# Squares summed by TensorE behind a stream, Down's banks in two groups, and a silu of one column ahead of each gate turn

## The reference

```python
# first_block, for l in range(2)
u = rms_norm(h, norm_pre_mix[l])
p = u @ w_in[l]                      # four mixers follow on slices of p
h = h + rms_norm(mixed @ w_out[l], norm_post_mix[l])
u = rms_norm(h, norm_pre_ffn[l])
ffn = (silu(u @ w_ffn_gate[l]) * (u @ w_ffn_up[l])) @ w_ffn_down[l]   # 2048 -> 5632 -> 2048
h = h + rms_norm(ffn, norm_post_ffn[l])
# second_block: one layer, attention of two kinds, then
x + gate * rms_norm_2(merged @ w_out, g_post)
```

## Time and profile before

| | us |
|---|---|
| median of 3 runs | 4174.72 |
| lowest, highest | 4172.66, 4178.52 |
| the profiled execution | 4183.72 |
| its span, first to last instruction | 4181.5 |
| PE busy | 3740.4 (89%) |
| PEld busy | 3315.9 (79%) |
| DVE busy | 2042.0 (49%) |
| ACT busy | 1763.6 (42%) |
| POOL busy | 1680.6 (40%) |
| mean granted TensorE clock | 0.945 |

### The profile page before, as it was taken

The page is one execution under the profiler, slowest core; times in us unless marked ns, Lnnn a source line. Parts: engine busy times, 40 slices in busy tenths (PEclk is TensorE's granted clock), DMA queues, the critical chain, the costliest instruction groups (busy, mean ns, idle before and its releaser), DMA issues. The chain is left out here.

```text
span 4181.5 us, 60673 instructions
## 1 busy us (share of the span) xinstructions
PE 3740.4 (89%) x25774; PEld 3315.9 (79%) x25774; DVE 2042.0 (49%) x2000; ACT 1763.6 (42%) x1700; POOL 1680.6 (40%) x663
## 2 busy tenths in 40 slices
PE   8788888799999998787888799999998889889988
PEld 7787787688888887776788688888887788878777
DVE  5536533555554555645532555555555433244464
ACT  4315333544443445415433544444445324544443
POOL 0425555399990000324555299993000124540000
PEclk9999899899999999998989899999999979999999
DMA  5413334477765554413334477775554623326443
GB/s 190 130 52 110 109 114 147 155 237 235 240 227 179 181 181 131 132 52 106 103 115 136 148 236 242 236 234 172 189 181 160 193 62 105 111 94 201 161 161 121
DMA packets 380728, 655.44 MB, mean 157 GB/s; under 512 B 14928, under 2 KB 192096, under 8 KB 379648
## 3 DMA queue, kind: packets, MB, share of 16 engines
q1 hardware_dynamic: 365632, 598.24, 44.0%
q0 software_dynamic: 14912, 54.53, 3.7%
HBM read 645.37 MB, written 6.29 MB: 156 GB/s over the span
## 5 line engine op out<-in xcount | busy, mean ns | idle before, releaser
L213 PE MATMUL ps<-x_parts,w_hi 128*128 128x512 f32 x6160 | 2205.2, 402 | 109.3 <-DVE w_lo L192 31.8
L184 ACT ACTIVATE w_hi<-weight_ring 128x2048 fp32r<-128x2048 f32 (+1 forms) x564 | 1065.9, 1890 | 1617.8 <-PE ps L214 1079.7
L214 PE MATMUL ps<-x_parts,w_lo 128*128 128x256 f32 x6160 | 1739.1, 282 | 0.0
L213 PEld LDWEIGHTS ps<-x_parts,w_hi 128*128 128x128 f32 x6160 | 1170.9, 190 | 414.7 <-issue 74.3
L192 DVE TENSOR_TENSOR w_lo<-weight_ring,w_hi 128x2048 fp32r<-128x2048 f32 x392 | 955.3, 2437 | 1078.9 <-ACT w_hi L184 1078.9
L192 POOL TENSOR_TENSOR w_lo<-weight_ring,w_hi 128x2048 fp32r<-128x2048 f32 (+1 forms) x172 | 791.8, 4607 | 1430.9 <-ACT w_hi L184 1430.9
L214 PEld LDWEIGHTS ps<-x_parts,w_lo 128*128 128x128 f32 x6160 | 1177.0, 191 | 0.0
L542 PE MATMUL ps<-x_parts,w_hi 128*128 128x256 f32 x2592 | 795.3, 307 | 138.6 <-POOL w_lo L192 75.4
L543 PE MATMUL ps<-x_parts,w_hi 128*128 128x256 f32 x2592 | 759.4, 293 | 0.0
L544 PE MATMUL ps<-x_parts,w_lo 128*128 128x256 f32 x2592 | 758.2, 293 | 0.0
L542 PEld LDWEIGHTS ps<-x_parts,w_hi 128*128 128x128 f32 x2592 | 524.0, 202 | 173.4 <-POOL w_lo L192 94.0
(11 more groups left out here) (393 smaller groups left out, 2637.0 us busy)
## 6 DMA issues: line engine op xcount, KB each, us to landing
weight_ring<-in_w_in SPq DMA_DIRECT2D x212, 1024.0 KB, 5.2
weight_ring<-in_w_ffn_gate SPq DMA_DIRECT2D x88, 1024.0 KB, 5.3
weight_ring<-in_w_ffn_up SPq DMA_DIRECT2D x88, 1024.0 KB, 5.2
weight_ring<-in_w_ffn_down SPq DMA_DIRECT2D x88, 1024.0 KB, 5.3
spare<-in_w_ada POOLq DMA_DIRECT2D x96, 512.0 KB, 5.0
weight_ring<-in_w_out SPq DMA_DIRECT2D x32, 768.0 KB, 4.5
weight_ring<-in_w_out SPq DMA_DIRECT2D x24, 1024.0 KB, 5.1
weight_ring<-in_w_br_a SPq DMA_DIRECT2D x8, 1024.0 KB, 5.1
```

Source lines behind the costliest of these rows:

```text
L184: core.nc.scalar.activation(core.w_hi[:, g % 2, at], core.ring[:, (self.start + g) % RING, at], ACT.Copy)\
L213: mm(out, hi, core.x_parts[:, x, :, :].rearrange("p a t -> p (a t)"), start=first, stop=False)
L214: return mm(out[:, 0:T], lo, core.x_hi[:, x, :], start=False, stop=last)
```

## The change

Three things.

*A silu of one column.* In Linear.ahead the ScalarE loop of the gate stream begins each trip with a Silu on one column of the constant ones, written to a tile "table" of its own that nobody reads.

*Down's banks in two groups.* In the first and the last slab of each half the products go group by group: banks 0 to 3 with both rows of tiles, then banks 4 to 7. The eighth product of a half's last slab raises first_banks_full; the first copy (L731) waits for that alone, the second for slab_used. VectorE no longer waits for slab_used there, only for the copies. The first slab of the second half waits for evacuated[0] ahead of its first product and for evacuated[1] ahead of its ninth.

*Squares.* Every quarter's squares get a place of their own (acc, sq, and x tiles 4 to 7 and 0 to 3), and VectorE's adds and folds are dropped. TensorE sums the squares of quarters 0, 1 and 2 in Post.tail, behind the last matmul of the stream and still in its block: 12 matmuls into bank 0, once that bank's last output has been read, the third group after a wait for quarter 2's squares. Only the four matmuls of quarter 3 are left for the next block. There ScalarE's order is now: square of quarter 3, L184 of slab 1, root, scales of quarters 2 and 3.

```diff
--- before.py
+++ after.py
@@ -289,12 +289,11 @@
                     self.post.early_square(eng, q - 1)
                     if q < 3:
                         self.post.scale(eng, q - 1, q)
-                elif self.post is not None and part == "low" and q == 2:
-                    self.post.early_sum(eng)
-                    self.post.fold(eng)
 
         if self.ahead_trips > 0:
             with eng.Fori(0, self.ahead_trips) as i:
+                if part == "high" and self.kind == "gate":
+                    self.core.nc.scalar.activation(self.core.table[:, :], self.core.const("ones")[:, 0:1], ACT.Silu)
                 for g in range(BODY):
                     step(g, i)
         for g in range(max(self.ahead_trips, 0) * BODY, self.n_slabs):
@@ -416,6 +415,9 @@
                             chunk(q, i)
                 for q in range(trips * self.body, self.total):
                     chunk(q, None)
+                if post is not None:
+                    pe.wait_ge(core.free[0].sem, core.free[0].base + (self.total - 2) // 2 + 2)
+                    post.tail(pe)
 
             @block.scalar
             def _(act):
@@ -664,6 +666,7 @@
         core, nc = self.core, self.core.nc
         evacuated = [core.sig("banks_read_0"), core.sig("banks_read_1")]
         copied = core.sig("cross_banks_copied")
+        first_banks = core.sig("first_banks_full")
         last = self.SLABS - 1
         self.begin(after)
 
@@ -690,16 +693,22 @@
 
                     pe.wait_ge(core.x_lo_ready.sem, core.x_lo_ready.base + g + 1 + (0 if i is None else i * 4))
                     s = g % self.SLABS
-                    for k in range(2):
-                        for m in range(8):
-                            if g == self.SLABS and k == 0 and m % 4 == 0:
-                                pe.wait_ge(*evacuated[m // 4].at(1))
-                            w = (g % 2, slice(k * 1024 + m * P, k * 1024 + m * P + P))
-                            mm = self.product(core.ps[:, m, :], w, 2 * (g % 4) + k, s == 0 and k == 0, s == last and k == 1)
+                    order = [(k, m) for k in range(2) for m in range(8)]
+                    if s in (0, last):
+                        order = [(k, 4 * b + m) for b in range(2) for k in range(2) for m in range(4)]
+                    for n, (k, m) in enumerate(order):
+                        if g == self.SLABS and n % 8 == 0:
+                            pe.wait_ge(*evacuated[n // 8].at(1))
+                        w = (g % 2, slice(k * 1024 + m * P, k * 1024 + m * P + P))
+                        mm = self.product(core.ps[:, m, :], w, 2 * (g % 4) + k, s == 0 and k == 0, s == last and k == 1)
+                        if s == last and n == 7:
+                            mm.then_inc(*first_banks.up())
                     mm.then_inc(core.slab_used, 1)
 
                 self.turns(pe, slab)
+                pe.wait_ge(*evacuated[0].at(2))
+                post.tail(pe)
 
             def ahead(eng, part, split, x_split, epilogue, early):
                 for g in range(2):
@@ -710,7 +719,6 @@
 
                 def step(g, i):
                     if g % self.SLABS == last:
-                        self.used(eng, g)
                         epilogue(g // self.SLABS)
                     if g + 2 < self.n_slabs:
                         split(eng, g + 2, i)
@@ -726,6 +734,10 @@
             def _(act):
                 def epilogue(h):
                     for b in range(2):
+                        if b == 0:
+                            act.wait_ge(*first_banks.at(h + 1))
+                        else:
+                            self.used(act, (h + 1) * self.SLABS - 1)
                         if h:
                             act.wait_ge(*evacuated[b].at(1))
                         nc.scalar.activation(core.tmp[:, b, :, :], core.ps[:, 4 * b:4 * b + 4, T:2 * T], ACT.Copy).then_inc(*copied.up())
@@ -754,12 +766,7 @@
                         nc.vector.tensor_tensor(self.dst[:, 8 * h + 4 * b:8 * h + 4 * b + 4, :], core.ps[:, 4 * b:4 * b + 4, 0:T],
                                                 core.tmp[:, b, :, :], ALU.add).then_inc(*evacuated[b].up())
 
-                def early(g):
-                    if g == self.n_slabs - 2:
-                        post.early_sum(dve)
-                        post.fold(dve)
-                ahead(dve, "low", self.low, self.x_low, epilogue, early)
+                ahead(dve, "low", self.low, self.x_low, epilogue, lambda g: None)
 
             block.gpsimd(pool)
 
@@ -975,6 +982,7 @@
         self.bounds = self.sb("bounds", [P, 3, GT])
         self.chunk_w = self.sb("chunk_w", [P, 4, 4])
         self.cs = self.sb("small_consts", [P, n_small])
+        self.table = self.sb("table", [P, 1])
 
     def second(self, name):
 
@@ -1027,17 +1035,15 @@
 
 
 
     def __init__(self, m, src, weight, x, acc, sq, reloaded=None):
         self.m, self.src, self.weight, self.x, self.reloaded = m, src, weight, x, reloaded
-        self.acc, self.sq = acc, sq
-        self.squares, self.summed, self.scaled = m.sig("squares"), m.sig("early_summed"), m.sig("scaled")
+        self.sq = [acc, sq, x[:, 4:8, :], x[:, 0:4, :]]
+        self.squares, self.scaled = m.sig("squares"), m.sig("scaled")
 
     def early_square(self, act, q):
 
-        if q == 2:
-            act.wait_ge(*self.summed.at(1))
-        to = self.acc if q == 0 else self.sq
-        self.m.nc.scalar.activation(to, self.src[:, QUARTERS[q], :], ACT.Square).then_inc(*self.squares.up())
+        self.m.nc.scalar.activation(self.sq[q], self.src[:, QUARTERS[q], :], ACT.Square).then_inc(*self.squares.up())
 
     def scale(self, act, q, squared=None):
 
@@ -1048,17 +1054,18 @@
             ins = self.m.nc.scalar.activation(x, x, ACT.Copy, scale=self.weight[:, k:k + 1])
         ins.then_inc(*self.scaled.up())
 
-    def early_sum(self, dve):
-        dve.wait_ge(*self.squares.at(2))
-        self.m.nc.vector.tensor_tensor(self.acc, self.acc, self.sq, ALU.add).then_inc(*self.summed.up())
-    def fold(self, dve):
-        m, acc = self.m, self.acc
-        dve.wait_ge(*self.summed.at(1))
-        done(dve, m.nc.vector.tensor_tensor(acc[:, 0:2, :], acc[:, 0:2, :], acc[:, 2:4, :], ALU.add), m.dve_step)
-        m.nc.vector.tensor_tensor(acc[:, 0, :], acc[:, 0, :], acc[:, 1, :], ALU.add)
+    def total(self, pe, q):
+        m = self.m
+        for k in range(4):
+            ins = m.nc.tensor.matmul(m.ps[:, 0, 0:T], m.const("ones"), self.sq[q][:, k, :], start=q == 0 and k == 0, stop=q == 3 and k == 3)
+        return ins
+    def tail(self, pe):
+        for q in range(3):
+            pe.wait_ge(*self.squares.at(q + 1))
+            self.total(pe, q)
 
 
 class Lead:
@@ -1098,10 +1105,8 @@
         if post is None:
             pe.wait_ge(*self.landed["ones"].all())
         else:
-            total(0, [post.acc[:, 0, :]], True, False)
-            total(0, [post.sq[:, k, :] for k in range(4)], False, False)
             pe.wait_ge(*self.squares.at(1))
-            total(0, [post.x[:, k, :] for k in range(4)], False, True).then_inc(*self.sums.up())
+            post.total(pe, 3).then_inc(*self.sums.up())
         if self.ada is not None:
             ada_part(0)
         if self.weight is None:
@@ -1145,13 +1150,13 @@
             ins.then_inc(*self.high.up())
 
         if post is not None:
-            nc.scalar.activation(post.x[:, 0:4, :], post.src[:, QUARTERS[3], :], ACT.Square).then_inc(*self.squares.up())
+            post.early_square(act, 3)
+            if stream is not None:
+                stream.high(act, 1)
+            act.wait_ge(*self.sums.at(1))
+            root_mean(m, m.ps[:, 0, 0:T], self.inv[:, 0, :], D).then_inc(*self.root.up())
             post.scale(act, 2)
             post.scale(act, 3, 1)
-            act.wait_ge(*self.sums.at(1))
-            root_mean(m, m.ps[:, 0, 0:T], self.inv[:, 0, :], D).then_inc(*self.root.up())
-            if stream is not None:
-                stream.high(act, 1)
         if self.weight is None:
             return
         for q in range(4):
```

## The result

| | median us | runs | ratio to the kernel before, 95% interval |
|---|---|---|---|
| before | 4176.22 | 5 | |
| after | 4145.95 | 5 | 0.9922 [0.9907, 0.9937] |

The direction held and each of the three parts did what it was made for, the size didn't. The profiled execution of the changed kernel took 4147.06 us with a span of 4145.2, granted clock 0.949 on the mean. In its listing the lines have moved: L296 is the new silu with its table load, L326, L335 and L349 were L327, L336 and L350, L355 was L356, L743 and L766 were L731 and L754, L1026 was L1018, L1046 squares a quarter, and L1061 are the sums on PE.

A forecast was written before the change was run, and what follows sets the result against it. The gate streams were taken as bound by TensorE, with short stalls for late splits, plus seam waits. Gains 12.9 + 5.8 + 3.1 = 21.8 us off the median 4174.72 gave 4152.9 us, range 4144 to 4166.

The forecast's parts named there:

- head stalls: Gate streams, TensorE stalls at 20 turn heads behind a 1.28 us table load: all go, 12.9 us gained.
- silu stalls: Gate streams, TensorE's 12 waits behind the silu L336, 7.1 us idle: expected to stay, no gain.
- Down's middle: Seam between Down's halves: TensorE idle 0.5 instead of 2.54 us, a slow-clock slab gone in layer 0; 5.8 us gained.
- squares on TensorE, at the seams: Stream ends: Sqrt 2.0 us earlier at out_ret, twice; 0.3 later at Down, twice, and the last stream; 3.1 us gained.
- rival 1: Gate streams: silu stalls spread from 12 to all 20 turns, 11.2 us back, gain 10.6, 4164.1 us; chance 0.10.
- all go: Gate turn heads: each stall, at most 1.02 us, is shorter than the 1.28 us removed, so all 20 vanish.
- added wait inside the first slab: Down's second half: bank group 1 is ready at 1441.2, TensorE wants it at 1442.2, so the wait is free.
- moves as a whole: Block behind each seam: only the DVE chain hangs on the Sqrt and shifts with it, with no further gain or loss.
- The base: Time the gain is subtracted from: median 4174.72 us, 9.0 below the profiled execution's 4183.72.
- rival 2: Gate turns: loads at L184 and L336 stay, the head gets a third; gain 8.9, 4165.8 us; chance 0.09.

The follow-up runs named there:

- Copy version: The kernel before plus a one-column ACT.Copy, in place of Silu, at the head of each gate turn: 4147.93 us, ratio 0.9931.
- The late silu on the kernel before: The kernel before with each silu moved behind ScalarE's next rounding (L184), no silu added at the head: 4159.34 us, ratio 0.9956.

## Why the prediction was wrong in size

The mean of two profiles each takes out some of the luck of one. Spans: 4176.4 before, 4145.0 after, 31.4 us apart.

| term | forecast | in the traces |
|---|---|---|
| head stalls | 12.9 | 15.2 (20 stalls of 0.76) |
| silu stalls | 0 | 6.8 (11.9 to 5.1) |
| Down's middle | 5.8 | 6.1 |
| squares on TensorE, at the seams | 3.1 | 4.6 |
| first pairs of the gate streams, at 1.2 GHz | none | -2.0 (3.0 to 5.0) |
| pace of the pairs | none | -1.1 (24.8 to 25.9) |
| elsewhere, not followed up | none | 1.8 |
| sum | 21.8 | 31.4 |

**The step that failed** is the sentence "What is late next is the silu stall, whose chain waits for no load", with "the head's stall does not feed the silu's" under rival 1. The chain does wait for no load, as the Copy version shows, but that doesn't make the stall independent of the heads: set at no gain, it gave 6.8 us. A silu stall comes when L192 ahead of L350 meets a GpSimd operation (2.29 us alone, 2.76 or more in 89 of 93 turns with a stall; with GpSimd's work cut none is left). How often it does differs: 12, 17, 15 and 17 of 22 in the four profiles with full GpSimd work, the silu in its old place and head stalls; 7, 7, 4, 6 and 8 in the five without head stalls. In the first group a turn takes 46.1 to 46.4 us on the mean of a stream and a GpSimd step (from one of its DMA issues to the next) 9.2 to 9.5, in the second 44.9 to 45.5 and 9.4 to 9.6. With nearly five steps in a turn, the same operation would meet the same L192 turn after turn; that this is why the first group stalls more is argued, no run sets the phase. The late silu on the kernel before shows two things more. It keeps its 20 head stalls, but without silu stalls its turns take 45.4 to 45.6 us, and there the L192 ahead of the addition took over 2.7 us in 6 of 22: so by this profile it isn't the stall at the head by itself that brings the meetings. And the heads lose only 1.6 us by it.

**The head term was mis-sized** by 2.3 us of 12.9. The count of 20 and "all go" held. The size came from idle times plus 0.16 hidden; start to start also shows a slower next interval (0.45 to 0.46 instead of 0.35 us), 0.1 at each head. And the reason given, a load of 1.28 us, is less than half of it: alone it costs 0.32 us, and the rest is again GpSimd's. The figure came out near since it was read from rows and not built from the load.

**Down's middle** held: 1.93 us less in each of the two gaps (0.5 expected, 0.56 to 0.61 found), and the stretch at 1.2 GHz behind it is gone in both layers. The added wait inside the first slab stayed free: its pairs run on at about 0.35 us. The slow stretch was counted in layer 0 only; in the second profile of the kernel before it stood in both, 4 and 5 pairs at 0.64 us. The share of the gain is 2.2 instead of 1.8.

**The seams.** The Sqrt of out_ret came 2.0 us earlier, Down's about 0.2 to 0.3 later, the last one's 0.2 later, all as worked out. But "moves as a whole" missed that the second sum of squares behind out_ret took 9.21 instead of 9.88 us, and the granted share between 787 and 790 us was 0.77 in place of 0.55. What brought the clock back sooner stays open: PE's last record ended at 778.2 before and 778.3 after, and it then idled 5.96 us in both. From the stream's last L213 to the gate stream's first, the whole seam is 2.7 us shorter, twice.

Part of that is paid back right behind it, and this the prediction didn't have. The gate stream starts at half clock, and it keeps it longer in the changed kernel. Windows on the first pairs in layer 0, before, then after:

```profile
800.10:803.40 3.30, 3.29 (x10) 2.81 (x11) 3.30 (x4) 1.06 (x1) 0.00 (x0) 0.51 0.00 0
```

```profile
799.50:805.00 5.50, 5.49 (x17) 4.72 (x18) 5.50 (x5) 3.24 (x3) 0.00 (x0) 0.50 0.01 3
```

5 pairs took about 0.64 us before, 9 after (5 and 7 in layer 1), 1.3 and 0.7 us more. It is so in every profile here: 4 or 5 such pairs where VectorE adds the squares, 7 or 9 where TensorE does. With it the squares' part is worth 2.6 us, a little less than the 3.1 forecast.

**The base.** The prediction took the median, 9.0 us below the profiled execution, and was right to: the two paces explain a profile 10 us off. Rival 1's silu stalls moved, but down instead of up, and rival 2's third load didn't come. The range's lower end was the forecast less all silu stalls as they were then counted, 9.0 us, with no error in any other term; 6.8 of the silus and 2.3 of the heads already use it up.

## What to carry to other kernels

A stall may have two causes that each look like the whole: here a table load or a place in the queue, and a GpSimd operation that happened to be running. Before a term is set to "unchanged", look at the durations of the instruction that is late (2.29 to 3.37 us for one shape says that something gets in its way at times) and give it a gain side. In an in-order queue, put what waits for another engine behind what the bottleneck waits for, if nobody needs it soon; here it cost nothing that shows, and no silu stall was left in three profiles while GpSimd worked in full. And before two profiles are compared by a few us, look at how far two profiles of one kernel lie apart.

## What the runs showed of the hardware beside this

- A running stream of L213/L214 pairs keeps one of two paces over long stretches, 0.3467 or 0.3533 us a pair, at a granted clock of 1.00, and mostly changes between them at a stall; 6000 pairs at the one or the other are 40 us apart (an estimate from the two), and 11.7 us of it was seen between two profiles. What sets it stays open.
- Where L192 on VectorE and a GpSimd operation meet, the second waits: L192 3.25 instead of 2.29 us in one place, GpSimd's addition 2.99 instead of 1.30 in the other.
- Eight records (1.99 us) after 1.52 us of idle time ran at full clock in both seams, while the earlier trace rows show half of it after 1.86 us.
- The first 5 pairs of a gate stream run at a granted clock of 0.51 in the kernel before, the first 9 at 0.50 in the changed one, behind an idle time of 6.05 us in both. What makes the difference stays open.
- A table load is 1.283 us in every row, and nothing stands between it and the ACTIVATE behind it.
